# Attention of a two-layer encoder: a score tile's exponential issued as three instructions, one for each PSUM bank

## The chip, the cores and the metric

The kernel runs on one core of one Trainium2 chip. The metric is the device time of one execution in microseconds (us). Engines are named as the profile names them: PE is TensorE (PEld its weight loads), ACT is ScalarE, DVE is VectorE, POOL is GpSimd, SP is SyncE, which issues the DMAs.

## What is computed

The model takes 1024 tokens of width 1024, puts 16 meta tokens ahead of them, and runs two layers: a mixer of Fourier transform and attention with a squared-ReLU MLP, then an HGRN2 mixer with a second such MLP. The change touches the attention of the first layer alone. Cut to that, the reference is:

```python
N_Q_HEADS, N_KV_HEADS, HEAD_DIM = 6, 2, 128
q = apply_rope(rms_norm(q, q_gain), cos, sin)      # 1040 tokens, 6 heads
k = apply_rope(rms_norm(k, k_gain), cos, sin)      # 1040 tokens, 2 heads
s = jnp.einsum('bqhgd,bkhd->bhgqk', qb, k).astype(jnp.float32) * scale
p = jax.nn.softmax(s, axis=-1).astype(v.dtype)
o = jnp.einsum('bhgqk,bkhd->bqhgd', p, v)
```

Every query sees all 1040 keys. Everything is float32.

## The kernel before, in words

The sequence is padded to T = 1044 = 3 x 348 columns (CB = 348) and to nine token blocks of TT = 116. Matrix products are made of float32 values split into a high and a low part (fp32r), three passes each: high x high, high x low, low x high. The order of work is written out by hand for each engine, with semaphores between them; there is no scheduler.

**Tiles of the attention.** A tile g is one block of 116 queries of one head against all keys: 6 x 9 = 54 tiles. Its scores fill three PSUM banks (`ps[:, 0..2]`, 348 columns each, the last 4 of the last bank masked). Step s of block b works on tile g = 6b + s. Each engine has its own `attend(b, s)`: steps of block 0 are written out, blocks 1 to 8 are a loop, block 9 empties the pipeline. `begun` and `drained` leave out what does not exist yet or any more. In one step the engines issue, in this order:

- PE (line 1310): waits for the exponential of tile g - 1 (line 1318), then 9 score matmuls of tile g, three to a bank, a signal after each bank (`a_s`, lines 1319 to 1324). Then 9 matmuls of probabilities x values of older tiles into banks 6 and 7 (line 1336). Then, after the wait for the scaled probabilities of tile g - 1 (`a_p`, line 1342), 9 transposes of tile g - 1 into banks 3 to 5, three to a bank (line 1347); from the second tile on each bank first waits until the low part of tile g - 2 has been taken out of it (`a_pl`, line 1345).
- DVE (line 871): `low(0)`, the low part of bank 3 of tile g - 2 (line 876), which waits for ACT's `high(0)` of that bank (`a_ph`). Then the maximum of each score bank (line 885, waits `a_s`), two one-column instructions that make the exponent's bias (lines 887 and 890, signal `a_nb`), `low(1)` and `low(2)`, in steps 1 and 4 the low part of a new query group (line 869), and last the reciprocal of the tile's sum (line 897), which waits for the exponential (line 896).
- ACT (line 564): the exponential of tile g, one instruction over the three banks into `prob`, whose row sum goes to `amax[:, 5]` (lines 573 and 574, waits `a_nb`). It shows in the trace as an ACTIVATE and an ACTIVATION_READ_ACCUMULATOR; the signal `a_exp` is on the second. Then `high(0)` of tile g - 1 (line 579, waits `a_t`), the scaling of `prob` by the reciprocal (line 585, waits `a_rc`, signals `a_p`), `high(1)` and `high(2)`, and in some steps one more copy (line 591 in steps 2 and 5, line 562 in steps 0 and 3).

So `high(0)` stands behind the exponential on ACT, and the first maximum stands behind `low(0)` on DVE. POOL and SP do nothing in this stage: the weights of the next one are already there.

The few lines that matter most:

```python
A(prob[s % 2][0:TT, :].rearrange("p (a b) -> p a b", b=CB), ps[0:TT, 0:3, 0:CB], ACT.Exp, bias=amax[0:TT, 4:5],
  scale=scale_of(qsc, b, s), accum_out=amax[0:TT, 5:6]).then_inc(a_exp, 1)
```

`bias` and `scale` are both columns in SBUF, one value for each partition.

Of the kernel before, what the change touches and what calls it, by code (L numbers as in the profile page):

```python
# [17 lines left out]
F32 = mybir.dt.float32  # L18
F32R = mybir.dt.float32r
U8 = mybir.dt.uint8  # L20
ALU = mybir.AluOpType
ACT = mybir.ActivationFunctionType
AX = mybir.AxisListType

P = 128
# [5 lines left out]
CB = 348  # L31
T = 3 * CB
TT = T // 9
# [42 lines left out]
def encoder(nc, x, meta, mix_gain, ab_w_in, q_gain, k_gain, ab_w_out, c_w_in, lb_logits, o_gain,  # L76
# [3 lines left out]
    with ctx:  # L80
# [4 lines left out]
        def at(name, shape, dt, offset):  # L85
            return nc.alloc_sbuf_tensor_at(name, shape, dt, offset=base + offset, align_bytes=4)
# [14 lines left out]
        o_c = o_t + 4 * row  # L101
# [5 lines left out]
        stat = at("stat", [P, 2, 9], F32, o_c + 1484)  # L107
        qsc = at("qsc", [P, NQ, 9], F32, o_c + 1484 + 72)
        nqsc = at("nqsc", [P, NQ, 9], F32, o_c + 1484 + 72 + 216)
        amax = at("amax", [P, 8], F32, o_c + 1484 + 72 + 432)  # L110
        e_c = o_c + 1484 + 72 + 432 + 32


        xst = at("xst", [P, 9, 1024], F32, o_x)
# [17 lines left out]
        prob = (at("prob0", [P, T], F32, o_x + 9216 + 50176), at("prob1", [P, T], F32, o_t + 9216))  # L132
# [35 lines left out]
        ps = ctx.enter_context(nc.psum_tensor("ps", [P, 8, 512], F32))  # L168

        def sem(name):  # L170
            return ctx.enter_context(nc.semaphore(name))
# [62 lines left out]
        a_mn = sem("two_banks_bias_ready")  # L234
        a_nb = sem("exp_bias_ready")
        a_exp = sem("exp_done")
        a_rc = sem("sum_inverse_ready")
        a_p = sem("probs_ready")
        a_t = sem("probs_transposed")
# [89 lines left out]
        def group_col(b, kv):  # L329
            return b * CB + kv * (GRP * T)  # L330

        def scale_of(table, b, s):

            flat = table[0:TT, :, :].rearrange("p a b -> p (a b)")
            return flat[:, bass.ds(b * 3 + ((s // 3) * GRP * 9 + s % 3), 1)]

        def begun(b, s, lag):

            return not isinstance(b, int) or b * 6 + s >= lag

        def drained(b, s, lag):

            return isinstance(b, int) and b * 6 + s - lag >= 3 * NG

        def tile_cols(t, s):

            return t[0:TT, (s // 3) % 2, :, (s % 3) * TT:(s % 3 + 1) * TT]

        def turned(r):
            return ps[0:TT, 3 + r, 0:3 * TT].rearrange("p (a b) -> p a b", b=TT)  # L350
# [131 lines left out]
        def _(act):  # L482
            A = nc.scalar.activation
# [50 lines left out]
            for jj in range(8):  # L534
# [17 lines left out]
              bias=eps[0:TT, :], scale=1.0 / HD).then_inc(r_qr, 1)  # L552
# [7 lines left out]
            def q_high(b, gg):  # L560

                A(qh[:, gg, :], yf[:, bass.ds(group_col(b, gg), CB)], ACT.Copy).then_inc(a_qh, 1)

            def attend(b, s):

                g = b * 6 + s
                if not drained(b, s, 0):

                    act.wait_ge(a_nb, g + 1)
                    if begun(b, s, 2):  # L570

                        act.wait_ge(a_t, b * 18 + (3 * s - 3))
                    A(prob[s % 2][0:TT, :].rearrange("p (a b) -> p a b", b=CB), ps[0:TT, 0:3, 0:CB], ACT.Exp, bias=amax[0:TT, 4:5],  # L573
                      scale=scale_of(qsc, b, s), accum_out=amax[0:TT, 5:6]).then_inc(a_exp, 1)

                def high(r):
                    if begun(b, s, 1) and not drained(b, s, 1):
                        act.wait_ge(a_t, b * 18 + (3 * s - 2 + r))
                        A(tile_cols(pth, s - 1)[:, 3 * r:3 * r + 3, :], turned(r), ACT.Copy).then_inc(a_ph, 1)

                high(0)
                if not drained(b, s, 0):

                    act.wait_ge(a_rc, g + 1)
                    A(prob[s % 2][0:TT, :], prob[s % 2][0:TT, :], ACT.Copy, scale=amax[0:TT, 6:7]).then_inc(a_p, 1)
                high(1)
                high(2)
                if s in (2, 5) and begun(b, s, 8):

                    act.wait_ge(a_pv, b * 2 + (s // 3 - 1))  # L590
                    A(yf[:, bass.ds(group_col(b - 1, s // 3), CB)], ps[:, 6 + s // 3, 0:CB], ACT.Copy).then_inc(a_ev, 1)
                if s in (0, 3) and not drained(b, s, 0):

                    q_high(b + s // 3, 1 - s // 3)
# [3 lines left out]
            for s in range(6):  # L598
                attend(0, s)
            with act.Fori(1, 9) as b:  # L600
                for s in range(6):
                    attend(b, s)
# [128 lines left out]
        def _(dve):  # L731
            V = nc.vector
# [79 lines left out]
            for ft in range(2):  # L812
                dve.wait_ge(f_b, 2 * ft + 2)
                for hm in range(2):
                    c = ps[:, ((5, 6), (1, 2))[ft][hm], :]
                    s = bsin[:, ft, hm, :]
# [54 lines left out]
            def attend(b, s):  # L871
                def low(r):
                    if begun(b, s, 2) and not drained(b, s, 2):
                        hi, lo = tile_cols(pth, s - 2), tile_cols(ptl, s - 2)
                        dve.wait_ge(a_ph, b * 18 + (3 * s - 5 + r))
                        V.tensor_tensor(lo[:, 3 * r:3 * r + 3, :], turned(r), hi[:, 3 * r:3 * r + 3, :], ALU.subtract).then_inc(a_pl, 1)

                low(0)
                if not drained(b, s, 0):


                    col = [amax[0:TT, c:c + 1] for c in range(8)]
                    for c in range(3):
                        dve.wait_ge(a_s, b * 18 + (3 * s + c + 1))
                        V.tensor_reduce(col[c], ps[0:TT, c, 0:CB], AX.X, ALU.max).then_inc(a_mx, 1)
                    dve.wait_ge(a_mx, b * 18 + (3 * s + 2))
                    V.scalar_tensor_tensor(col[3], col[0], col[1], scale_of(nqsc, b, s), ALU.max, ALU.mult).then_inc(a_mn, 1)
                    dve.wait_ge(a_mx, b * 18 + (3 * s + 3))
                    dve.wait_ge(a_mn, b * 6 + (s + 1))
                    V.scalar_tensor_tensor(col[4], col[2], scale_of(nqsc, b, s), col[3], ALU.mult, ALU.min).then_inc(a_nb, 1)  # L890
                low(1)
                low(2)
                if s in (1, 4) and not drained(b, s, 0):
                    q_low(b + s // 4, 1 - s // 4)
                if not drained(b, s, 0):
                    dve.wait_ge(a_exp, b * 6 + (s + 1))
                    V.reciprocal(col[6], col[5]).then_inc(a_rc, 1)


# [265 lines left out]
        def _(pe):  # L1165
# [144 lines left out]
            def attend(b, s):  # L1310

                gg, i = s // 3, s % 3
                if not drained(b, s, 0):
                    if i == 0:
                        pe.wait_ge(a_ql, b * 2 + (gg + 1))
                    if begun(b, s, 1):

                        pe.wait_ge(a_exp, b * 6 + s)
                    for c in range(3):
                        n = CB if c < 2 else CB - (T - TOK)  # L1320
                        for q, k in ((qh, kh), (qh, kl), (ql, kh)):
                            ins = M(ps[0:TT, c, 0:n], q[:, gg, i * TT:(i + 1) * TT], k[:, gg, c * CB:c * CB + n],  # L1322
                                    start=(q is qh and k is kh), stop=(q is ql))
                        ins.then_inc(a_s, 1)

                p = (s - 2) % 3
                if begun(b, s, 5 + p) and not drained(b, s, 5 + p - 2):
                    jg, jb = ((s - 5 - p) // 3) % 2, (s - 5 - p) // 6
                    if p == 0:
                        pe.wait_ge(a_pl, b * 18 + 3 * (s - 2))  # L1330
                        if begun(b, s, 5 + 6):

                            pe.wait_ge(a_ev, (b + jb) * 2 + (jg - 1))
                    for c in range(3 * p, 3 * p + 3):
                        for v, w in ((vth, pth), (vth, ptl), (vtl, pth)):
                            ins = M(ps[:, 6 + jg, 0:CB], v[0:TT, jg * 9 + c, :], w[0:TT, jg, c, :], start=(c == 0 and v is vth and w is pth),
                                    stop=(c == 8 and v is vtl))
                    if p == 2:
                        ins.then_inc(a_pv, 1)
                if begun(b, s, 1) and not drained(b, s, 1):  # L1340

                    pe.wait_ge(a_p, b * 6 + s)
                    for r in range(3):
                        if begun(b, s, 2):
                            pe.wait_ge(a_pl, b * 18 + (3 * s - 5 + r))
                        for j in range(3 * r, 3 * r + 3):
                            ins = nc.tensor.transpose(ps[0:TT, 3 + r, (j % 3) * TT:(j % 3 + 1) * TT], prob[(s - 1) % 2][0:TT, j * TT:(j + 1) * TT], ident[0:TT, 0:TT])
                        ins.then_inc(a_t, 1)
# [289 lines left out]
```

## Time and profile before

| what | value |
|---|---|
| time, median of 3 runs | 3040.42 us (3037.49 to 3046.72) |
| the profiled execution: its time | 3046.08 us |
| its span in the profile | 3044.3 us |
| PE busy | 2865.9 us, 94% of the span |
| DVE busy | 1500.1 us, 49% |
| ACT busy | 690.5 us, 23% |
| POOL busy | 921.4 us, 30% |
| attention (first scores to last copy) | 240.5 to 476.3 us of the span |

The profile is one execution on the chip. Busy shares are averages over stages with different limits; the attention is 8% of the span. Starts are us from the span's start. An instruction's duration runs from its start to its end; the next one on the same engine can start before that end, so the distance between two starts is what an engine's queue really costs. Matmul ends are modelled.

### The profile page before, as it was taken

How to read it: one execution, taken by the hardware profiler on the slowest of the kernel's cores; microseconds unless marked ns; L12 is line 12 of the kernel's file. 1: busy time of each engine (PE TensorE's matmuls, PEld its weight loads, DVE VectorE, ACT ScalarE, POOL GpSimd, SP SyncE). 2: the span in 40 equal slices, each digit the busy share in tenths (PEclk: the TensorE clock that was granted, in tenths of full speed). 3: DMA queues.
4: the chain of work that ended last, by engine and by line, in shares of the span. 5: the costliest groups of instructions: out<-in, count | busy, mean ns of one | idle time of the engine just before them, and what ended most of it. 6: DMA issues, size and time to landing. Idle time of an engine off the chain costs nothing.

```text
span 3044.3 us, 40709 instructions
## 1 busy us (share of the span) xinstructions
PE 2865.9 (94%) x16501; PEld 2630.7 (86%) x16501; DVE 1500.1 (49%) x1832; ACT 690.5 (23%) x968; POOL 921.4 (30%) x396
## 2 busy tenths in 40 slices
PE   7998999999999999998999998998778999999998
PEld 6897999999999999998888888897766888888887
DVE  6377885431222222356867767768655322222224
ACT  3117883210000110121221221221223111000012
POOL 2230002343434434332222222222113444444442
PEclk9998999999999999999999999999888999999999
DMA  4010001111111111110000000000001111111111
GB/s 144 28 35 1 0 0 28 44 47 49 43 49 49 42 49 46 45 51 27 28 28 28 28 28 28 26 29 24 18 14 28 49 49 48 45 44 48 49 49 70
DMA packets 169438, 116.79 MB, mean 38 GB/s; under 512 B 3715, under 2 KB 163797, under 8 KB 169335
## 3 DMA queue, kind: packets, MB, share of 16 engines
q1 hardware_dynamic: 169190, 114.70, 12.5%
q8 instruction: 87, 1.43, 0.2%
q10 hardware_dynamic: 144, 0.53, 0.1%
q14 instruction: 17, 0.13, 0.0%
HBM read 111.03 MB, written 4.19 MB: 38 GB/s over the span
## 4 chain that ended last, share of the span: by engine, by line
PE 79%; DVE 12%; issue 5%; ACT 2%; DMA 0%; SPq 0%; DVEq 0%; ACTq 0%
PE ps L1196 67%; PE ps L1322 3%; PE ps L1461 3%; PE ps L1416 2%; DVE aa L1029 1%; DVE kk L1049 1%; PE ps L1484 1%; DVE h L922 1%; DVE kk L1048 1%; PE ps L1428 1%; ACT prob L573 1%; PE ps L1272 1%; DVE fd L1056 1%; DVE qq L1052 1%; DVE tmp L785 0%
## 5 line engine op out<-in xcount | busy, mean ns | idle before, releaser
L1196 PE MATMUL ps<-xh,wsp 128*128 128x348 f32 (+1 forms) x5056 | 1068.3, 340 | 18.2 <-DVE xl L771 12.2
L469 POOL TENSOR_TENSOR wsp<-raw,ones 128x1024 fp32r<-128x1024 f32 x196 | 387.5, 1977 | 2068.6 <-PE ps L1196 2049.2
L1196 PEld LDWEIGHTS ps<-xh,wsp 128*128 128x128 f32 x5056 | 860.9, 190 | 69.1 <-issue 18.6
L1196 PE MATMUL ps<-xl,wsp 128*128 128x348 f32 (+1 forms) x2528 | 593.6, 338 | 0.0
L1196 PE MATMUL ps<-ah,wsp 128*128 128x348 f32 (+1 forms) x2560 | 567.4, 350 | 0.0
L471 POOL TENSOR_TENSOR wsp<-raw,wsp 128x1024 fp32r<-128x1024 f32 x196 | 533.8, 2723 | 15.4
L1196 PEld LDWEIGHTS ps<-ah,wsp 128*128 128x128 f32 x2560 | 444.0, 188 | 44.7
L1196 PEld LDWEIGHTS ps<-xl,wsp 128*128 128x128 f32 x2528 | 441.4, 190 | 23.0
L1196 PE MATMUL ps<-al,wsp 128*128 128x348 f32 (+1 forms) x1280 | 323.1, 350 | 0.0
L618 ACT ACTIVATE tmp<-tmp 128x1044 f32<-128x1044 f32 (+1 forms) x64 | 68.5, 1071 | 1099.5 <-DVE tmp L939 559.0
L922 DVE TENSOR_TENSOR h<-h,ps 128x1024 f32<-128x1024 f32 x128 | 154.9, 1219 | 246.9 <-PE ps L1196 245.3
L1196 PEld LDWEIGHTS ps<-al,wsp 128*128 128x128 f32 x1280 | 225.7, 188 | 23.2
L923 DVE TENSOR_TENSOR h<-h,ps 128x1044 f32<-128x1044 f32 x72 | 89.3, 1240 | 256.5 <-PE ps L1196 256.5
L939 DVE SCALAR_TENSOR_TENSOR tmp<-ps,rms 128x1044 f32<-128x1044 f32 x32 | 39.9, 1246 | 278.2 <-PE ps L1196 275.4
L1461 PE MATMUL ps<-qq,kp 128*128 128x128 f32 (+1 forms) x960 | 136.8, 296 | 40.6 <-DVE qq L1052 26.1
L1461 PEld LDWEIGHTS ps<-qq,kp 128*128 128x128 f32 (+1 forms) x960 | 126.8, 201 | 52.8 <-issue 22.3
L937 DVE SCALAR_TENSOR_TENSOR tmp<-ps,rms 128x1024 f32<-128x1024 f32 x32 | 39.2, 1225 | 265.6 <-PE ps L1196 262.8
L679 ACT ACTIVATE kp<-kk 128x520 f32<-128x520 f32 (+1 forms) x112 | 66.5, 643 | 383.6 <-PE ps L1461 203.8
L943 DVE TENSOR_TENSOR al<-tmp,ah 128x1044 fp32r<-128x1044 f32 (+1 forms) x64 | 151.8, 2372 | 2.9 <-ACT ah L620 1.9
L1196 PE MATMUL ps<-oh,wsp 128*128 128x512 f32 x256 | 89.4, 452 | 39.6 <-DVE h L922 34.6
L1029 DVE COPY_PREDICATED aa<-msk,ps 128x512 f32<-128x512 uint8 x168 | 92.4, 589 | 53.6 <-PE ps L1461 52.6
L1196 PEld LDWEIGHTS ps<-oh,wsp 128*128 128x128 f32 x256 | 50.9, 212 | 62.0 <-DVE h L922 45.9
(181 smaller groups left out, 2986.4 us busy)
## 6 DMA issues: line engine op xcount, KB each, us to landing
raw<-in_w SPq DMA_DIRECT2D x128, 512.0 KB, 4.0
raw<-in_c_w_in SPq DMA_DIRECT2D x40, 512.0 KB, 3.7
raw<-in_ab_w_in SPq DMA_DIRECT2D x12, 512.0 KB, 3.8
xst<-in_x SPq DMA_DIRECT2D x8, 512.0 KB, 7.6
raw<-in_ab_w_out SPq DMA_DIRECT2D x8, 512.0 KB, 3.7
raw<-in_c_w_out SPq DMA_DIRECT2D x8, 512.0 KB, 3.2
out<-ost SPq DMA_DIRECT2D x16, 256.0 KB, 3.5
tabs<-in_dft_tok SPq DMA_DIRECT2D x2, 856.4 KB
```

The lines of the kernel that those rows point to most:

```text
L469: nc.gpsimd.tensor_tensor(wsp[:, slot, 0, :], raw[:, slot, :], one, ALU.mult).then_inc(w_high, 1)
L471: nc.gpsimd.tensor_tensor(wsp[:, slot, 1, :], raw[:, slot, :], wsp[:, slot, 0, :], ALU.subtract).then_inc(w_split, 1)
L618: A(tmp[:, j % 2, t0:t1], tmp[:, j % 2, t0:t1], ACT.Square).then_inc(l_s, 1)
L679: ins = A(dst, src, ACT.Copy)
L922: return V.tensor_tensor(real_pieces(h[:, k, :]), real_pieces(h[:, k, :]), real_outp(s), ALU.add).then_inc(z_free, 1)
L923: return V.tensor_tensor(pieces(h[:, k, :]), pieces(h[:, k, :]), outp(s), ALU.add).then_inc(z_free, 1)
L943: V.tensor_tensor(al[:, c0, j, t0:t1], tmp[:, j % 2, t0:t1], ah[:, c0, j, t0:t1], ALU.subtract).then_inc(l_l, 1)
L1029: V.copy_predicated(aa[0:rows, c0:c0 + n, 0:rows], mask, bank).then_inc(h_le, 1)
L1196: ins = M(ps[:, 3 * s + c, 0:n], w(a, k), b(k)[:, c0:c0 + n], start=(k == first and a == 0 and b is xa), stop=(k == last and a == 1))
L1322: ins = M(ps[0:TT, c, 0:n], q[:, gg, i * TT:(i + 1) * TT], k[:, gg, c * CB:c * CB + n], start=(q is qh and k is kh), stop=(q is ql))
L1416: ins = M(dst, left, right, start=(b == 0), stop=(b == len(parts) - 1))
L1461: ins = M(ps[0:n, 6 + (r0 + r) % 2, a * P:a * P + n], left, right, start=True, stop=True)
```

## The change

The one exponential of a tile becomes three, one for each bank of 348 columns, each with a sum of its own (columns 7 to 9 of `amax`, which grows from 8 to 10 columns). Each of them signals `a_exp`, so the semaphore counts 18 in a block, not 6. PE waits ahead of each bank of scores for the exponential of the same bank of the tile before. DVE waits for the third exponential, adds the three sums into column 5 with a new reduction, signals a new semaphore `a_sm`, waits for it, and then takes the reciprocal.

```diff
--- before.py
+++ after.py
@@ -107,8 +107,8 @@
         stat = at("stat", [P, 2, 9], F32, o_c + 1484)
         qsc = at("qsc", [P, NQ, 9], F32, o_c + 1484 + 72)
         nqsc = at("nqsc", [P, NQ, 9], F32, o_c + 1484 + 72 + 216)
-        amax = at("amax", [P, 8], F32, o_c + 1484 + 72 + 432)
-        e_c = o_c + 1484 + 72 + 432 + 32
+        amax = at("amax", [P, 10], F32, o_c + 1484 + 72 + 432)
+        e_c = o_c + 1484 + 72 + 432 + 40
 
 
         xst = at("xst", [P, 9, 1024], F32, o_x)
@@ -234,6 +234,7 @@
         a_mn = sem("two_banks_bias_ready")
         a_nb = sem("exp_bias_ready")
         a_exp = sem("exp_done")
+        a_sm = sem("sum_of_banks_ready")
         a_rc = sem("sum_inverse_ready")
         a_p = sem("probs_ready")
         a_t = sem("probs_transposed")
@@ -570,8 +571,9 @@
                     if begun(b, s, 2):
 
                         act.wait_ge(a_t, b * 18 + (3 * s - 3))
-                    A(prob[s % 2][0:TT, :].rearrange("p (a b) -> p a b", b=CB), ps[0:TT, 0:3, 0:CB], ACT.Exp, bias=amax[0:TT, 4:5],
-                      scale=scale_of(qsc, b, s), accum_out=amax[0:TT, 5:6]).then_inc(a_exp, 1)
+                    for c in range(3):
+                        A(prob[s % 2][0:TT, c * CB:(c + 1) * CB], ps[0:TT, c, 0:CB], ACT.Exp, bias=amax[0:TT, 4:5],
+                          scale=scale_of(qsc, b, s), accum_out=amax[0:TT, 7 + c:8 + c]).then_inc(a_exp, 1)
 
                 def high(r):
                     if begun(b, s, 1) and not drained(b, s, 1):
@@ -879,7 +881,7 @@
                 if not drained(b, s, 0):
 
 
-                    col = [amax[0:TT, c:c + 1] for c in range(8)]
+                    col = [amax[0:TT, c:c + 1] for c in range(7)]
                     for c in range(3):
                         dve.wait_ge(a_s, b * 18 + (3 * s + c + 1))
                         V.tensor_reduce(col[c], ps[0:TT, c, 0:CB], AX.X, ALU.max).then_inc(a_mx, 1)
@@ -893,7 +895,9 @@
                 if s in (1, 4) and not drained(b, s, 0):
                     q_low(b + s // 4, 1 - s // 4)
                 if not drained(b, s, 0):
-                    dve.wait_ge(a_exp, b * 6 + (s + 1))
+                    dve.wait_ge(a_exp, b * 18 + (3 * s + 3))
+                    V.tensor_reduce(col[5], amax[0:TT, 7:10], AX.X, ALU.add).then_inc(a_sm, 1)
+                    dve.wait_ge(a_sm, b * 6 + (s + 1))
                     V.reciprocal(col[6], col[5]).then_inc(a_rc, 1)
 
 
@@ -1313,10 +1317,10 @@
                 if not drained(b, s, 0):
                     if i == 0:
                         pe.wait_ge(a_ql, b * 2 + (gg + 1))
-                    if begun(b, s, 1):
-
-                        pe.wait_ge(a_exp, b * 6 + s)
                     for c in range(3):
+                        if begun(b, s, 1):
+
+                            pe.wait_ge(a_exp, b * 18 + (3 * s - 2 + c))
                         n = CB if c < 2 else CB - (T - TOK)
                         for q, k in ((qh, kh), (qh, kl), (ql, kh)):
                             ins = M(ps[0:TT, c, 0:n], q[:, gg, i * TT:(i + 1) * TT], k[:, gg, c * CB:c * CB + n],
```

## Rows read from the trace of the kernel before

**Rows 1.** Window from third to last exponential: PE, PEld, DVE, ACT, POOL busy; PEclk, DMA

```profile
254.36:465.45 211.09, 203.88 (x1355) 188.40 (x1356) 174.38 (x477) 185.96 (x338) 0.00 (x0) 1.00 0.00 0
```

**Rows 2.** Waits between 265 and 465 us: engine, line, releaser: us, times, longest

```profile
DVE amax L897 <- ACT prob L573: 23.7, 48, 0.7
ACT prob L573 <- DVE amax L890: 23.4, 48, 0.8
PEld ps L1322 <- ACT prob L573: 15.0, 48, 0.4
```

**Rows 3.** Timeline of ACT, one step: start, us, engine, line, operation

```profile
332.96 1.22 ACT L573 ACTIVATE prob<-ps,amax,qsc 116x1044 f32<-116x1044 f32 x1 [0.35 <-DVE amax L890]
334.08 0.19 ACT L573 ACTIVATION_READ_ACCUMULATOR prob<-ps,amax,qsc 116x1 f32 x1
334.17 0.45 ACT L579 ACTIVATE pth<-ps 116x348 fp32r<-116x348 f32 x1
334.51 1.17 ACT L585 ACTIVATE prob<-prob,amax 116x1044 f32<-116x1044 f32 x1
335.58 0.80 ACT L579 ACTIVATE pth<-ps 116x348 fp32r<-116x348 f32 x2
336.25 0.50 ACT L562 ACTIVATE qh<-y 128x348 fp32r x1
337.09 1.22 ACT L573 ACTIVATE prob<-ps,amax,qsc 116x1044 f32<-116x1044 f32 x1 [0.33 <-DVE amax L890]
```

**Rows 4.** Timeline of DVE, the same step

```profile
332.60 0.22 DVE L890 SCALAR_TENSOR_TENSOR amax<-amax,nqsc 116x1 f32<-116x1 f32 x1
332.74 0.94 DVE L876 TENSOR_TENSOR ptl<-ps,pth 116x348 fp32r<-116x348 f32 x2
334.30 0.16 DVE L897 RECIPROCAL amax<-amax 116x1 f32<-116x1 f32 x1 [0.62 <-ACT prob L573]
334.65 0.52 DVE L876 TENSOR_TENSOR ptl<-ps,pth 116x348 fp32r<-116x348 f32 x1 [0.19 <-ACT pth L579]
335.10 1.47 DVE L885 TENSOR_REDUCE amax<-ps 116x1 f32<-116x348 f32 x3
336.48 0.21 DVE L887 SCALAR_TENSOR_TENSOR amax<-amax,nqsc 116x1 f32<-116x1 f32 x1
336.73 0.22 DVE L890 SCALAR_TENSOR_TENSOR amax<-amax,nqsc 116x1 f32<-116x1 f32 x1
```

**Rows 5.** Timeline of PE, the same step

```profile
333.17 1.08 PE L1347 MATMUL ps<-ident,prob 116*116 116x116 f32 x9
334.32 0.42 PE L1322 MATMUL ps<-kh,qh 128*116 128x348 f32 x1
...
334.74 0.32 PE L1322 MATMUL ps<-kh,ql 128*116 128x348 f32 x1
...
335.69 0.32 PE L1322 MATMUL ps<-kh,ql 128*116 128x344 f32 x1
```

**Rows 6.** The chain that ended last, the start of the attention

```profile
244.50 1.32 ACT prob L573 x2
...
254.36 1.31 ACT prob L573 x2
...
259.83 0.36 ACT pth L579
260.21 0.52 DVE ptl L876
260.74 1.39 DVE amax L885 x3
```

**Rows 7.** Lines of ACT: instructions and durations in ns, min/median/max

```profile
L610 ACT ACTIVATE mh<-y x8: 1057/1058/1072, 476.3 to 483.1; 128x1044 fp32r<-128x1044 f32 x8
```

**Rows 8.** The same of line 562

```profile
L562 ACT ACTIVATE qh<-y x19: 473/503/505, 238.8 to 460.5; 128x348 fp32r x16, 128x348 fp32r<-128x348 f32 x3
```

**Rows 9.** Timeline of PE, transposes of the last tile

```profile
468.22 0.41 PE L1347 MATMUL ps<-ident,prob 116*116 116x116 f32 x2
```

## The prediction

> **What bounds the kernel now.** I asked first what a microsecond lost in this stage is worth. In the window from the third exponential to the last, POOL is idle, no DMA runs, and PE is busy 203.9 of 211.1 us at a granted clock of 1.00, the upper level of 2.4 GHz [rows 1]. Nothing from outside can be late here, the next stage's weights are there, and everything after it needs the attention: a step's gain or loss goes to the end undiminished. The window holds 51 distances between exponentials, 4.14 us each; in the step read below it is 337.09 - 332.96 = 4.13 us [rows 3].
>
> The list of waits gives the ring: DVE and PE wait for the exponential, the exponential waits for the bias [rows 2]. The timelines of the three engines place it. I count from the start E of an exponential (332.96).
>
> - ACT: E 0; sum read 1.12; high(0) 1.21, to 1.66; scaling 1.55; high(1) 2.62; a further copy 3.29 [rows 3].
> - DVE: reciprocal 1.34; low(0) 1.69, 0.03 after high(0) ends; first maximum 2.14; bias instructions 3.52 and 3.77; next exponential 4.13, 0.36 after the second [rows 3, 4].
> - PE: next scores at 1.36, 0.05 after the sum's read ends, and PE had been idle for 0.30, the average of the wait list (15.0/48) [rows 2, 3, 5].
>
> Two chains reach the first maximum together. By PE, bank 0 ends at 334.74 + 0.32 = 335.06. By ACT and DVE, exponential, high(0), low(0), and 0.44 later DVE is free: 335.09. The maximum starts at 335.10 [rows 4, 5]. After it PE is a little slower: its banks come 0.475 apart ((1.47 - 0.52)/2), while DVE left alone spaces maxima 0.435 ((1.39 - 0.52)/2), as in the chain at the stage's start, which indeed runs high, low, maximum [rows 4, 6]. So the PE chain bounds the step at 4.13, and **the ACT-DVE chain stands only 0.08 behind it, at 4.05**. The change frees the first and loads the second.
>
> **The change part by part.**
>
> *The wait of PE, bank by bank.* After the change bank 0 is released when the first sum is read, about E + 0.78. PE cannot use all of that: its transposes wait for low(1) and low(2), which end at 333.68, E + 0.72, and the last three follow; PE is free at 334.32 - 0.30, E + 1.06 [rows 4, 5]. The scores start 0.30 earlier. Bank 2 is released at about E + 2.02 and PE reaches it at 1.06 + 1.06 = 2.12: no wait. Gain on the PE chain 0.30 us, on the step at most the 0.08.
>
> *The exponential in three.* The elements are the same, two more instructions and two more sum reads come. An ACT instruction costs 0.84 ns for an element, from copies of 1044 and 348 columns: (1058 - 473)/696 [rows 7, 8]. From exponential to sum read are 1.12 us, less 1044 x 0.84 = 0.88: 0.24 fixed; from the read to the next start 0.09 [rows 3]. Two more: 2 x (0.24 + 0.09) = 0.67 us. All of it stands ahead of high(0), which starts at E + 1.88. Bounds of the fixed part: with the 503 ns of the loop's copies the slope is 0.80 and the fixed part 0.29, together 0.76; with the 450 ns of high(0), which reads PSUM as the exponential does, 0.87 and 0.21, together 0.60 [rows 3, 7, 8]. The low extreme is two high copies 0.35 apart, only 0.06 more than their elements [rows 3]: 0.30 together. I take 0.67, since the exponential has its own row. A gain is excluded: ACT only gets more to do.
>
> On this price the Trainium skill ("ScalarE: Activation LUTs", What ACT_TABLE_LOAD costs) says that an ACTIVATE with a bias column has about 280 ns beside its elements, one more such column adds 93, and neighbours overlap by 93. By that the fixed part is 0.28, the sum of the change +34 us and the time 3074; the page gives 1.24 us for our exponential and the row shows 1.22, so they agree. It is a rule against this change, and it also gives a reason for the 0.24.
>
> *The added reduction and its wait.* The third sum is ready at E + 1.97; the reduction starts at 2.00. A reduction of three elements is not in the trace: below it lies the reciprocal, 0.16, above it the one-column 0.21 of the bias and far above the 0.52 of a 348-column maximum [rows 4]. I take 0.17. The reciprocal then starts at 2.20, and low(0) can follow 0.14 later, as low(1) does after the bias: 2.34 [rows 4]. It would wait for high(0) until 1.88 + 0.45 + 0.03 = 2.36 anyway. Its cover is thus thin: with 0.21 it costs 0.02 a step, 1 us in all, with 0.52 it costs 0.34, 17 us.
>
> *What is queued behind.* On ACT the scaling moves from E + 1.55 to 2.41, high(1) to 3.48, high(2) to 3.82, the further copy to 4.16; ACT is free by about 4.55. PE's transposes need the scaled tile from E + 3.93 at the earliest and have it at 3.57. On DVE low(0) moves from 1.69 to 2.36, and the first maximum with it.
>
> *The new step.* 4.13 + 0.67 - 0.08 = 4.72 us: low(0) at 2.36, maxima from 2.80 spaced 0.435, bias, next exponential. It is the ACT-DVE chain, 4.05 + 0.67. ACT is free at 4.55, PE's own work is 4.13 - 0.30 = 3.83: neither bounds. 51 x 0.59 = **+30.0 us**.
>
> *Both ends.* From the first exponential to the third (9.86 us [rows 6]) there is no high or low yet, and the scores gain up to 0.6 in each of two distances; but the scaled tile, 0.86 later, holds the transposes ahead of the third scores. I take -0.4, between -1.2 and +0.5. At the end the last tile's transposes (468.22 [rows 9]) wait for its scaling, 0.86 later: +0.8. Sum: 30.0 - 0.4 + 0.8 = **+30.4 us**. The profiled execution took 3046.1 us, so its like would take 3076.5; the median shown is 5.7 below it, and against it I forecast 3040.4 + 30.4 = 3070.8.
>
> **The rivals.**
>
> *Serial sums.* An exponential that accumulates might not start until the sum before has been read: 0.19 after the read's start and not 0.09. No row shows two accumulating instructions in a row. Two gaps, +0.20 a step, +10: 3081.
>
> *Cheap pieces.* If the fixed part hides behind the piece before, as between two high copies, the pieces add 0.30: (0.30 - 0.08) x 51 = +11: 3051. Against it: the exponential's 0.24 is itself measured between starts.
>
> *PE sets the pace.* PE's row says that it waits 0.30 in each step for the exponential and for nothing else; freed, the step would be 3.83: -0.30 x 51 - 1 = -16, 3024. It decides where high(0) comes less than 0.08 later than now; and even with no delay at all the ACT-DVE chain stops the gain at 0.08 a step, -4. It would need my reading of rows 4, low(0) just ahead of the maximum, to be an accident of timing. Against it: the order on DVE is fixed in the code, and the chain at the start runs that way [rows 6].
>
> *The signals come together.* If the early exponentials' signals reached PE only with the third, the change would not do what it says. Scores at 2.02, banks again spaced by PE: 4.80 a step, +34, 3075. It lies within the main case's range.
>
> *The clock.* PE will idle 0.9 of 4.7 us, in one gap before its second group of transposes. If the clock fell to 1.2 GHz in this stage, the 3.83 would double: +3 us a step, at worst 150. Against it: the clock is 1.00 throughout the window, whose first steps have no value matmuls at all, 18 matmuls and not 27 [rows 1].
>
> **How the numbers follow.** The main case has 0.76 with the joined signals, its own range 3067 to 3076; serial sums 0.10; cheap pieces 0.07; PE's pace 0.03; the clock or something not seen, 0.04. The range takes in main case and serial sums with the spread of the runs (3037 to 3047) about them: 3059 to 3085. A measurement tells 0.3% from no change, 9 us. Slower 0.92 (main, serial, most of cheap pieces, clock), same 0.05, faster 0.03.
>
> **What the profile after would show.** Each exponential 0.64 us long, starts 0.63 apart; high(0) 1.88 after the first; the reduction about 0.17; low(0) at 2.36, directly ahead of the maxima, now 0.435 apart; exponentials of neighbouring tiles 4.72 apart. PE's wait ahead of the scores gone, and a new one of about 0.85 ahead of its transposes, for DVE's line 876. I am wrong if the first sum read comes before E + 0.45 or the next exponential starts over 0.15 after it, if low(0) waits for the reciprocal and not for high(0), or if the granted clock leaves 1.00.

## The result

| | before | changed |
|---|---|---|
| median, first comparison | 3041.93 us (3037.49 to 3046.72, 4 runs) | 3080.78 us (3077.23 to 3084.12, 4 runs) |
| ratio | | 1.0127, 95% interval 1.0111 to 1.0143 |
| median, second comparison | 3040.15 us (17 runs) | 3073.92 us (3069.01 to 3076.84, 4 runs) |
| ratio | | 1.0111, 95% interval 1.0090 to 1.0131 |
| span of the profiled execution | 3044.3 us | 3081.0 us |

The change makes the kernel slower, by 39 us in the first comparison and by 34 us in the second. The forecast was 3071, 30 us slower, with a range from 3059 to 3085.

One step of the changed kernel on ACT, from E = 338.25. It answers to [rows 3].

```profile
338.25 0.64 ACT L575 ACTIVATE prob<-ps,amax,qsc 116x348 f32<-116x348 f32 x1 [0.42 <-DVE amax L892]
338.79 0.19 ACT L575 ACTIVATION_READ_ACCUMULATOR prob<-ps,amax,qsc 116x1 f32 x1
338.88 0.63 ACT L575 ACTIVATE prob<-ps,amax,qsc 116x348 f32<-116x348 f32 x1
...
340.03 0.20 ACT L575 ACTIVATION_READ_ACCUMULATOR prob<-ps,amax,qsc 116x1 f32 x1
340.12 0.46 ACT L581 ACTIVATE pth<-ps 116x348 fp32r<-116x348 f32 x1
340.65 1.17 ACT L587 ACTIVATE prob<-prob,amax 116x1044 f32<-116x1044 f32 x1
...
342.93 0.64 ACT L575 ACTIVATE prob<-ps,amax,qsc 116x348 f32<-116x348 f32 x1
```

The pieces last 0.64 us and start 0.63 apart; the sum read comes 0.54 after each start and the next instruction 0.09 later. `high(0)` starts at E + 1.87, not at 1.21, and the next exponential at 4.68, not 4.13.

The same step on DVE [rows 4]:

```profile
340.26 0.16 DVE L899 TENSOR_REDUCE amax<-amax 116x1 f32<-116x3 f32 x1 [1.29 <-ACT prob L575]
340.45 0.16 DVE L901 RECIPROCAL amax<-amax 116x1 f32<-116x1 f32 x1
340.61 0.52 DVE L878 TENSOR_TENSOR ptl<-ps,pth 116x348 fp32r<-116x348 f32 x1
341.05 1.36 DVE L887 TENSOR_REDUCE amax<-ps 116x1 f32<-116x348 f32 x3
...
342.57 0.22 DVE L892 SCALAR_TENSOR_TENSOR amax<-amax,nqsc 116x1 f32<-116x1 f32 x1
```

Reduction at E + 2.01, reciprocal at 2.20, `low(0)` at 2.36 and the maxima directly behind it, 0.42 apart ((1.36 - 0.52)/2). DVE paces itself from `low(0)` on.

The timeline of PE in the same step [rows 5]:

```profile
338.60 0.94 PE L1351 MATMUL ps<-ident,prob 116*116 116x116 f32 x6 [0.53 <-DVE ptl L878]
339.31 0.39 PE L1326 MATMUL ps<-kh,qh 128*116 128x348 f32 x1
...
342.29 0.46 PE L1351 MATMUL ps<-ident,prob 116*116 116x116 f32 x3
343.28 0.94 PE L1351 MATMUL ps<-ident,prob 116*116 116x116 f32 x6 [0.53 <-DVE ptl L878]
```

And the list of waits of the changed kernel between 265 and 495 us, which answers to [rows 2]:

```profile
DVE amax L899 <- ACT prob L575: 55.7, 48, 1.4
PEld ps L1351 <- DVE ptl L878: 36.0, 47, 0.9
...
ACT prob L575 <- DVE amax L892: 11.3, 24, 1.0
DVE ptl L878 <- ACT pth L581: 2.5, 7, 0.4
```

The scores start at E + 1.06, as forecast, and hardly ever wait for an exponential any more (2.3 us in the whole stage, against 15.0). In their place PE waits 0.77 us a step (36.0/47) in the middle of its transposes, for the low parts of line 878. The wait has changed its name and more than doubled. Little of `high(0)` shows in the list, because DVE's reciprocal ends at 340.61 and `high(0)` at 340.58: DVE is held by the two together and is never seen idle for the second alone.

The granted clock did not stay at 1.00 from the third exponential to the last, as it had in the kernel before [rows 1]:

```profile
251.77:494.96 243.19, 213.51 (x1359) 188.08 (x1359) 177.12 (x528) 225.50 (x543) 0.00 (x0) 0.99 0.00 0
```

The lower level (1.2 GHz) falls into the first steps alone: 0.85 between 255 and 270 us, 1.00 from 270 us on.

Where the time is, by parts of the two profiles:

| part | before, us | changed, us | difference |
|---|---|---|---|
| first scores to first exponential | 4.0 | 4.0 | 0 |
| tiles 0 to 6 (six distances) | 26.4 | 28.8 | +2.4 |
| tiles 6 to 53: 40 steps within the loop | 4.13 each | 4.68 each | +22.2 |
| the 7 steps across the loop's end among them | 4.21 each | 5.13 each | +6.4 |
| last exponential to the copies of the next stage | 10.9 | 11.8 | +0.9 |
| **attention** | **235.8** | **267.7** | **+31.9** |
| MLP and the rest up to the second mixer | 858.5 | 858.3 | -0.2 |
| HGRN2 mixer | 935.6 | 942.0 | +6.4 |

31.9 us lie in the attention. Another 6.4 are the mixer's, which the change does not touch (see the second profile, below). What lies ahead of the attention, untouched too, was 1.5 us shorter (239.0 for 240.5), so the spans differ by 36.7.

### The profile page after: what moved, and what is told of

Its sections match the earlier page's. It is cut to its first block, busy times and chain, and to the rows that moved or that the text cites. A ratio compares the mean times of both kernels' runs of the same rounds, so it can differ in the third digit from the quotient of the medians.

```text
span 3081.0 us, 41043 instructions
## 1 busy us (share of the span) xinstructions
PE 2879.5 (93%) x16501; PEld 2630.0 (85%) x16501; DVE 1501.9 (49%) x1886; ACT 732.6 (24%) x1184; POOL 919.3 (30%) x396
## 4 chain that ended last, share of the span: by engine, by line
PE 79%; DVE 14%; issue 4%; ACT 2%; DMA 0%; SPq 0%; DVEq 0%; ACTq 0%
PE ps L1200 67%; PE ps L1465 3%; PE ps L1326 2%; DVE amax L887 2%; PE ps L1420 2%; PE ps L1351 1%; DVE aa L1033 1%; DVE kk L1053 1%; DVE h L926 1%; PE ps L1488 1%; DVE kk L1052 1%; DVE ptl L878 1%; ACT prob L575 1%; DVE qq L1056 1%; PE ps L1432 1%
## 5 line engine op out<-in xcount | busy, mean ns | idle before, releaser
L472 POOL TENSOR_TENSOR wsp<-raw,wsp 128x1024 fp32r<-128x1024 f32 x196 | 532.4, 2716 | 15.4
```

Of the source, the lines that this page charges most:

```text
L472: nc.gpsimd.tensor_tensor(wsp[:, slot, 1, :], raw[:, slot, :], wsp[:, slot, 0, :], ALU.subtract).then_inc(w_split, 1)
```

## The experiments

Starts are again counted from the first exponential of a step, E. "Attention" is the time from the first scores to the first copy of the next stage (line 610 in the kernel before), 235.8 us before and 267.7 after the change. Times are medians, set against the kernel before in the same comparison: 3040.78 us (23 runs) for the first four experiments, 3040.15 us (17 runs) for the others. The steps across the loop's end are those between two turns; the eight turns give seven of them.

### One wait of PE instead of three

```diff
+                    if begun(b, s, 1):
+                        pe.wait_ge(a_exp, b * 18 + 3 * s)
                     for c in range(3):
-                        if begun(b, s, 1):
-
-                            pe.wait_ge(a_exp, b * 18 + (3 * s - 2 + c))
```

> The changed kernel with one thing undone: PE waits once, for the third exponential of the tile before, as it did for the only one. Theory (the step is set by ACT and DVE: exponentials, high, low, maxima): the scores start at E + 2.03 (the third sum read ends at 1.98) instead of 1.05, the first maximum stays at 2.80, but the maxima then follow PE's banks, 0.475 apart and not 0.43: 4.78 us a step for 4.68, +0.10 in 43 steps, nothing in the 8 at the loop's end. About +4 us on the changed kernel: 3085. That is all that the waits by bank are worth. Rival (the waits by bank disturb PE and are part of the loss): faster than the changed kernel, 3075 or less. Rival (PE's earlier start is worth much and the loss would be far larger without it): +0.3 or more a step, 3095 or more.

Measured: 3082.2 us, +41.4 on the kernel before (1.0132, 1.0111 to 1.0152). By the times it can't be told from the changed kernel (3080.8 us); the rows tell them apart. Steps of 4.79, and 5.13 across the loop's end. The row of its first score matmul in PE's timeline, in the step with E = 338.61:

```profile
340.62 0.42 PE L1325 MATMUL ps<-kh,qh 128*116 128x348 f32 x1 [0.74 <-ACT prob L575]
```

And its maxima in DVE's timeline, in the same step:

```profile
341.39 1.47 DVE L887 TENSOR_REDUCE amax<-ps 116x1 f32<-116x348 f32 x3
```

The scores start 0.95 later than in the changed kernel, at 2.01, and the step pays 0.11 for it: the first maximum stands at 2.78 (2.80 in the changed kernel), and only the maxima's spacing goes from 0.42 to 0.48 ((1.47 - 0.52)/2). That is all that the finer waits are worth once the exponential is in pieces. The attention took 276.8 us, 9 more than in the changed kernel and not 4: five lie between tiles 0 and 6, where the granted clock was lower. The window of this kernel from its first exponential to its seventh (columns: stretch, its length, then busy us and instructions of PE, PEld, DVE, ACT and POOL, the granted clock as a share of 2.4 GHz, DMA):

```profile
236.70:270.84 34.14, 26.35 (x117) 23.16 (x118) 20.20 (x58) 24.86 (x60) 0.00 (x0) 0.64 0.00 0
```

The same window of the changed kernel:

```profile
243.00:271.82 28.82, 22.01 (x120) 18.75 (x120) 19.27 (x58) 24.86 (x60) 0.00 (x0) 0.88 0.00 0
```

0.64 against 0.88. PE idles for long in these steps in both kernels (7.8 and 6.8 us), which have few matmuls of probabilities and values or none. Whether the single wait or the spread between executions made the difference, one profile of this kernel can't tell.

### The added reduction alone

```diff
-                      scale=scale_of(qsc, b, s), accum_out=amax[0:TT, 5:6]).then_inc(a_exp, 1)
+                      scale=scale_of(qsc, b, s), accum_out=amax[0:TT, 7:8]).then_inc(a_exp, 1)
...
                     dve.wait_ge(a_exp, b * 6 + (s + 1))
+                    V.tensor_reduce(col[5], amax[0:TT, 7:10], AX.X, ALU.add).then_inc(a_sm, 1)
+                    dve.wait_ge(a_sm, b * 6 + (s + 1))
                     V.reciprocal(col[6], col[5]).then_inc(a_rc, 1)
```

The two columns beside the sum hold zeros.

> The kernel before with one exponential, and the added reduction over three columns (two of them zero) with its semaphore alone. Theory: the reciprocal starts at E + 1.53 instead of 1.34, low(0) could follow at 1.67 and waits for high(0) until 1.69 anyway: steps of 4.13 as before. At the loop's end DVE's branch stands between reciprocal and low(0) (0.41 to 0.55 us there): those 8 steps get 0.2 to 0.3 longer. Together +2 us: 3044. Rival (reduction and wait lie on the step's path): 0.2 in each of 53 steps, +10: 3052.

Measured: 3043.0 us, +2.2 (1.0011, 1.0001 to 1.0020); attention 238.1 us, +2.3. Steps of 4.125 as before, 4.46 across the loop's end instead of 4.21. These seven account for 1.7 us; most of the rest lies in the first distance of all, 5.35 for 4.50 us. The timeline of DVE in an ordinary step (E = 322.54):

```profile
323.87 0.16 DVE L899 TENSOR_REDUCE amax<-amax 116x1 f32<-116x3 f32 x1 [0.63 <-ACT prob L574]
324.06 0.16 DVE L901 RECIPROCAL amax<-amax 116x1 f32<-116x1 f32 x1
324.22 0.52 DVE L878 TENSOR_TENSOR ptl<-ps,pth 116x348 fp32r<-116x348 f32 x1
```

And in one across the loop's end (E = 334.93):

```profile
336.44 0.16 DVE L901 RECIPROCAL amax<-amax 116x1 f32<-116x1 f32 x1
336.96 0.52 DVE L878 TENSOR_TENSOR ptl<-ps,pth 116x348 fp32r<-116x348 f32 x1 [0.35 <-ACT pth L580]
```

In the ordinary step `low(0)` starts 0.16 after the reciprocal, at E + 1.68, as before. Across the loop's end 0.52 lie between the two: DVE's branch stands there (its row is shown under "Why the prediction was right"). So the reduction costs nothing in the ordinary steps of the kernel before, where PE sets the pace; it costs 0.25 at each of the seven loop ends.

### A spare copy ahead of `high(0)`, or ahead of `high(2)`

```diff
                 def high(r):
                     if begun(b, s, 1) and not drained(b, s, 1):
                         act.wait_ge(a_t, b * 18 + (3 * s - 2 + r))
+                        if r == 0:
+                            if begun(b, s, 2):
+                                act.wait_ge(a_dm, b * 6 + (s - 1))
+                            A(rot[0:TT, 0:CB].rearrange("p (a b) -> p a b", b=TT), turned(r), ACT.Copy).then_inc(a_dm, 1)
                         A(tile_cols(pth, s - 1)[:, 3 * r:3 * r + 3, :], turned(r), ACT.Copy).then_inc(a_ph, 1)
```

The second kernel has `r == 2` in the added line. `a_dm` is a new semaphore; ACT waits for its last count ahead of the next stage.

> The kernel before, with one spare ACT copy of 348 columns in each step, just ahead of high(0), into memory that nobody reads. It costs ACT 0.34 us. Theory: high(0), low(0) and the first maximum come 0.34 later; that chain stood 0.08 behind PE's, so the step becomes 4.39: +0.26 in 43 steps, +0.18 in the 8 at the loop's end, which have a bubble to cover: +12.6 us, 3054.5. Rival (what counts is ACT's load, wherever it stands): the same as the spare copy behind, whatever that is. Rival (PE's wait for the exponential sets the step, the high and low parts do not): no change, 3042.

Measured: 3059.3 us, +18.5 (1.0061, 1.0045 to 1.0078); steps of 4.37, attention 249.1 us, +13.3. The attention agrees with the theory's +12.6, but the times lie above it: +12.6 is 1 us below their interval's lower end, +13.7. The profiled execution is the fastest of the five. ACT's timeline in the step with E = 332.04, the spare copy and `high(0)`:

```profile
333.26 0.45 ACT L583 ACTIVATE rot<-ps 116x348 f32<-116x348 f32 x1
333.60 0.46 ACT L584 ACTIVATE pth<-ps 116x348 fp32r<-116x348 f32 x1
```

DVE's timeline, `low(0)` and the maxima:

```profile
334.10 0.52 DVE L882 TENSOR_TENSOR ptl<-ps,pth 116x348 fp32r<-116x348 f32 x1 [0.54 <-ACT pth L584]
334.53 1.36 DVE L891 TENSOR_REDUCE amax<-ps 116x1 f32<-116x348 f32 x3
```

`low(0)` has gone from 1.69 to 2.06, and the maxima follow it without a gap, 0.42 apart.

> The kernel before, with the same spare ACT copy just ahead of high(2). Theory: high(2) ends at E + 3.76, low(2) needs it at 4.34; ACT is free at about 4.0 and the next exponential is due at 4.13: no change, 3042 (3040 to 3044). Rival (ACT's load counts): +0.34 in each step, up to +17, 3059, or the same as the copy ahead.

Measured: 3042.4 us, +1.6 (1.0002, 0.9989 to 1.0014); steps of 4.12, attention 236.4 us. ACT at the end of the step with E = 327.44:

```profile
330.39 0.46 ACT L583 ACTIVATE rot<-ps 116x348 f32<-116x348 f32 x1
330.73 0.47 ACT L584 ACTIVATE pth<-ps 116x348 fp32r<-116x348 f32 x1
...
331.56 1.22 ACT L574 ACTIVATE prob<-ps,amax,qsc 116x1044 f32<-116x1044 f32 x1
```

The same instruction with the same 0.34 us of ACT time costs 13 us in one place and nothing that shows in the other. This is the experiment that decides between the theory and ACT's load: what counts in this kernel is what stands between the exponential and `high(0)`.

### Two pieces instead of three

```diff
-                    for c in range(3):
-                        A(prob[s % 2][0:TT, c * CB:(c + 1) * CB], ps[0:TT, c, 0:CB], ACT.Exp, bias=amax[0:TT, 4:5],
-                          scale=scale_of(qsc, b, s), accum_out=amax[0:TT, 7 + c:8 + c]).then_inc(a_exp, 1)
+                    for i, (c0, c1) in enumerate(((0, 2), (2, 3))):
+                        A(prob[s % 2][0:TT, c0 * CB:c1 * CB].rearrange("p (a b) -> p a b", b=CB), ps[0:TT, c0:c1, 0:CB], ACT.Exp, bias=amax[0:TT, 4:5],
+                          scale=scale_of(qsc, b, s), accum_out=amax[0:TT, 7 + i:8 + i]).then_inc(a_exp, 1)
```

PE waits ahead of banks 0 and 2, and the reduction adds two sums.

> The exponential in two instructions, banks 0 and 1 together and bank 2 alone, with a wait of PE ahead of bank 0 and of bank 2, and the added reduction over two sums; everything else as in the changed kernel. Theory (fixed part and sum read of each further piece delay high(0)): one further piece, 0.33 us; high(0) at E + 1.55, low(0) at 2.03, step 4.05 + 0.33 = 4.38 (0.25 more than before in 43 steps) and about 4.75 at the loop's end (0.5 more in 8, for DVE's branch and the reduction): +15 us, 3056. Rival (the loss comes from splitting as such, whatever the number): near the changed kernel, 3080.

Measured: 3059.1 us, +18.9 (1.0060, 1.0044 to 1.0076); steps of 4.35, 4.80 across the loop's end, attention 252.6 us, +16.7. ACT in the step with E = 328.72:

```profile
328.72 0.93 ACT L575 ACTIVATE prob<-ps,amax,qsc 116x696 f32<-116x696 f32 x1 [0.42 <-DVE amax L892]
...
330.26 0.45 ACT L581 ACTIVATE pth<-ps 116x348 fp32r<-116x348 f32 x1
...
333.07 0.93 ACT L575 ACTIVATE prob<-ps,amax,qsc 116x696 f32<-116x696 f32 x1
```

`high(0)` at 1.54, 0.33 later than with one piece; with three it was 0.66 later. The price goes by the piece.

### The same two pieces in another order

```diff
+                for i, (c0, c1) in enumerate(((0, 2), (2, 3))):
+                    if not drained(b, s, 0):
+                        A(prob[s % 2][0:TT, c0 * CB:c1 * CB].rearrange("p (a b) -> p a b", b=CB), ps[0:TT, c0:c1, 0:CB], ACT.Exp, bias=amax[0:TT, 4:5],
+                          scale=scale_of(qsc, b, s), accum_out=amax[0:TT, 7 + i:8 + i]).then_inc(a_exp, 1)
+                    if i == 0:
+                        high(0)
+                high(1)
+                high(2)
                 if not drained(b, s, 0):
                     act.wait_ge(a_rc, g + 1)
                     A(prob[s % 2][0:TT, :], prob[s % 2][0:TT, :], ACT.Copy, scale=amax[0:TT, 6:7]).then_inc(a_p, 1)
-                high(1)
-                high(2)
...
                     for c in range(3):
+                        if c == 1:
+                            inverse()
                         dve.wait_ge(a_s, b * 18 + (3 * s + c + 1))
```

`inverse()` is the reduction and the reciprocal of tile g - 1, taken from the end of DVE's step.

> The two pieces again, reordered: on ACT high(0) between the two exponentials, high(1) and high(2) ahead of the scaling; on DVE reduction and reciprocal of the last tile between the first and the second maximum of the next one. The same instructions, no more and no fewer. Theory: low(0) at E + 1.40 is off the path; PE is free at 1.06 and its first bank ends at 1.80; reduction and reciprocal push the later maxima back by 0.3, so the next exponential is due at about 4.10, and ACT, with the further copy in two of three steps, is free at 4.15. Steps of about 4.13, no loss at the loop's end: 3042 (3037 to 3047), 14 us under the same pieces in the old order. Rival (three engines' work has grown, so the order hardly matters): within 4 us of the two pieces in the old order.

Measured: 3045.6 us, +5.4 on the kernel before, not told apart from it (1.0007, 0.9994 to 1.0019), and 13.5 under the same pieces in the old order. Steps of 4.00 to 4.12, 4.38 across the loop's end; attention 233.6 us, 2.2 less than before. ACT's timeline in the step with E = 323.74:

```profile
323.74 0.93 ACT L582 ACTIVATE prob<-ps,amax,qsc 116x696 f32<-116x696 f32 x1 [0.20 <-DVE amax L906]
...
324.67 0.45 ACT L578 ACTIVATE pth<-ps 116x348 fp32r<-116x348 f32 x1
325.01 0.65 ACT L582 ACTIVATE prob<-ps,amax,qsc 116x348 f32<-116x348 f32 x1
...
327.82 0.92 ACT L582 ACTIVATE prob<-ps,amax,qsc 116x696 f32<-116x696 f32 x1
```

DVE's timeline in the same step, `low(0)`, the first maximum and the reciprocal:

```profile
325.15 0.52 DVE L880 TENSOR_TENSOR ptl<-ps,pth 116x348 fp32r<-116x348 f32 x1 [0.69 <-ACT pth L578]
325.59 0.52 DVE L901 TENSOR_REDUCE amax<-ps 116x1 f32<-116x348 f32 x1
...
326.21 0.16 DVE L889 RECIPROCAL amax<-amax 116x1 f32<-116x1 f32 x1
```

The last score matmul of the first bank, in PE's timeline:

```profile
325.23 0.32 PE L1334 MATMUL ps<-kh,ql 128*116 128x348 f32 x1
```

`high(0)` has come forward from 1.21 to 0.93, `low(0)` from 1.69 to 1.41 and the first maximum from 2.14 to 1.85. That maximum still stands directly behind `low(0)`, and PE's first bank is ready 0.04 before it (325.55): the two chains arrive together again, so `low(0)` is not off the path as the theory has it. ACT goes from one instruction to the next without a pause in this step, and between 265 and 455 us it waits for DVE's bias only 16 times, 3.4 us in all. This is the fastest attention of the study, by the profile, but the whole kernel's time shows no gain. The profiled execution, 3036.0 us, lies 9.6 us below the median of the eleven.

### The three pieces in that order

The same edit on the changed kernel, with `high(0)` after the first of three pieces.

> The changed kernel's three exponentials, reordered in the same way: high(0) after the first piece, high(1) and high(2) ahead of the scaling, reduction and reciprocal between the first and the second maximum of the next tile. Theory: the place of high(0) makes the loss, not the 0.67 us of ACT time; ACT then becomes the bound: 1.87 for the three pieces, 1.03 for the high copies, 1.07 for the scaling, 0.37 for the further copy in two of three steps: 4.34 in those, about 4.15 in the others, 4.28 on average: +0.14 in 51 steps, 3049 (3044 to 3056), some 30 us under the changed kernel. Rival (the ACT time itself is the loss): near 3080.

Measured: 3055.5 us, +15.4 (1.0049, 1.0031 to 1.0068); steps of 4.22 to 4.37, 4.38 across the loop's end; attention 244.0 us, +8.2 on the kernel before and 23 under the changed kernel's second profile. By the times it is 18 under the changed kernel, where some 30 were expected. The step with E = 328.51 on ACT:

```profile
328.51 0.64 ACT L582 ACTIVATE prob<-ps,amax,qsc 116x348 f32<-116x348 f32 x1
...
332.54 0.48 ACT L595 ACTIVATE y<-ps 128x348 f32 x1
332.88 0.67 ACT L582 ACTIVATE prob<-ps,amax,qsc 116x348 f32<-116x348 f32 x1
```

ACT is busy from end to end: 332.88 - 328.51 = 4.37. The steps are near the theory's (4.34 with a further copy, 4.15 without), and its +7 us is near the attention's +8. The whole time is higher than that, by an amount that the profiled execution (span 3048.3, only 4 above the profile before) does not show; why the timed runs lie higher stays open.

### The changed kernel once more

> The changed kernel unaltered, for a second profile and times on the same chip as the three others. In the first profile the attention was 32 us longer and the stage of the HGRN2 mixer 6 us longer, with 7 us more at TensorE's lower clock in it. Theory: attention again 32 us longer (steps of 4.68 and about 5.1 at the loop's end), the mixer's stage anywhere between 932 and 942 us, as in the profiles of kernels that differ from the one before by a copy. Rival (the change lengthens the later stage too): the mixer's stage again at 940 us or more.

Measured: 3073.9 us, +33.8. Steps of 4.68, 5.12 across the loop's end, attention 266.8 us, +31.0. The mixer's stage in the profiles of the kernel before, the changed kernel and this one (windows, columns as above). Before:

```profile
1334.80:2270.40 935.60, 835.55 (x5257) 776.85 (x5256) 639.53 (x834) 217.39 (x321) 221.98 (x90) 0.95 0.09 26
```

The changed kernel, first profile:

```profile
1365.00:2307.00 942.00, 839.38 (x5257) 778.53 (x5256) 640.28 (x833) 217.33 (x321) 220.36 (x90) 0.95 0.09 25
```

The changed kernel, second profile:

```profile
1358.80:2294.60 935.80, 836.18 (x5257) 776.79 (x5255) 637.32 (x833) 217.31 (x320) 221.34 (x90) 0.96 0.09 26
```

935.6, 942.0 and 935.8 us: the second profile of the changed kernel has none of the first one's 6 us. In the other seven kernels the stage took 931.8 to 940.7 us, in no order that follows the attention. It is a spread between executions; an effect of the change on it is not seen. The mixer's is not the only one: the stretch ahead of the attention, the same in all ten but for one small memset in the second experiment, took 233.2 to 240.5 us (239.0 and 233.8 in the two profiles of the changed kernel). That leaves 31 to 32 us for the change itself: within the interval of the second comparison (27 to 40 us), and 2 us below the lower end of the first (34 to 43 us). In the profiled execution of the first the mixer's 6.4 us came on top; the other timed runs have no profile.

## Why the prediction was right

- **The two chains.** The reading that the ACT-DVE chain stood 0.08 behind PE's is borne out: a delay of 0.34 ahead of `high(0)` cost 0.25 a step (4.37 for 4.125), the same 0.34 behind cost nothing.
- **The exponential in three.** The forecast fixed part of 0.24 and 0.09 for the read give starts 0.63 apart and `high(0)` at 1.88; the rows show 0.63 and 1.87. The Trainium skill ("ScalarE: Activation LUTs", What ACT_TABLE_LOAD costs) gives 0.28 for the fixed part, 0.04 above the row, and says nothing of the sum's read. The rival of serial sums is out: the next accumulating instruction starts 0.09 after the read's start, while that read still runs.
- **The reduction.** Forecast 0.17, measured 0.16, and free in the ordinary step of the kernel before, as its own experiment shows. `low(0)` stands at 2.36, as forecast. In the changed kernel it is a tie: DVE goes on to `low(0)` 0.16 after the reciprocal starts, which is when `high(0)` lets it go as well. The prediction would be wrong "if low(0) waits for the reciprocal and not for high(0)"; the rows can't tell the two apart, and by this reading a longer reduction would have cost time.
- **The step.** Forecast 4.72, measured 4.68. The difference is the spacing of the maxima and what follows them: from the first maximum to the next exponential 1.88 us, forecast 1.92. Over the 40 ordinary steps between tiles 6 and 53 that is 1.4 us less than forecast (22.2 for 23.6).
- **PE.** Scores at 1.06 and one gap before the second group of transposes, both as forecast. The rival that PE sets the pace is out, and so is that of signals which come together: even with a single late wait the step is only 0.11 longer.
- **The step that was missing** is the loop. The sum used 51 equal distances. Across the loop's end DVE's branch puts 0.52 us between reciprocal and `low(0)`; before, the wait for `high(0)` hid nearly all of it, 0.41 against the 0.35 of an ordinary step [rows 4]. The changed kernel moves the reciprocal by 0.86 and `high(0)` by 0.66, and the branch comes out: 5.13 us for 4.68. DVE's timeline at that place, in the kernel before:

```profile
292.91 0.16 DVE L897 RECIPROCAL amax<-amax 116x1 f32<-116x1 f32 x1 [0.63 <-ACT prob L573]
293.32 0.52 DVE L876 TENSOR_TENSOR ptl<-ps,pth 116x348 fp32r<-116x348 f32 x1 [0.24 <-ACT pth L579]
```

And in the changed kernel:

```profile
354.50 0.16 DVE L901 RECIPROCAL amax<-amax 116x1 f32<-116x1 f32 x1
355.02 0.52 DVE L878 TENSOR_TENSOR ptl<-ps,pth 116x348 fp32r<-116x348 f32 x1 [0.35 <-ACT pth L581]
```

Between the two starts 0.41 before and 0.52 after. `low(0)` is at E + 2.72 there (E = 352.30), 0.36 later than in an ordinary step. The other 0.08 of the 5.13 is not new: from the second bias instruction to the next exponential ACT needs 0.44 across the loop's end and 0.36 within it, which is why the kernel before has 4.21 there for 4.13. The branch itself, in the list of the loop's own instructions in the changed kernel (durations in ns, then first and last start):

```profile
L909 DVEq COMPARE_BRANCH  x8: 50/56/67, 297.5 to 497.2; - x8
```

The first of the eight, at 297.5, stands between a reciprocal at 297.40 and a `low(0)` at 297.94. The prediction priced the reduction's cover as thin, 0.02 a step, and did not ask what else used the same cover; the reduction alone already lets 0.25 of the branch out (4.46 for 4.21). What the steps across the loop's end lose beyond the ordinary ones is (0.92 - 0.55) x 7 = 2.6 us of the 31.9, and 2.3 us beyond the forecast's 0.59 a step. A loop with fewer turns was not tried.
- **The ends.** Forecast -0.4 and +0.8. At the start the first two distances shrank by 1.1 us (8.8 for 9.9) and the next four grew by 3.5, where 4 x 0.59 = 2.4 was forecast: +2.4 for the six against a forecast of +2.0. In the second profile the same parts gave -0.4 and +2.5. At the end +0.9.
- **The clock.** The prediction called itself wrong if the granted clock left 1.00, and it did, to 0.99. The four distances in which it fell are the 5.35, 4.65, 5.24 and 4.81 us behind the third exponential; in the second profile they were 5.00, 4.64, 4.65 and 4.81. So at most some 1.3 us of the 31.9 belong to it, an estimate from 5.35 and 5.24 against 4.65. The rival's collapse of the clock through the whole stage did not come.
- **The sum.** Forecast +30.4, in the attention +31.9 and +31.0. That it is so close is in part luck: the ordinary steps' 1.4 us too much and the 2.3 us of the loop that were missing nearly cancel. The times gave +39 and +34. The 7 and 3 above the attention's are within what the mixer's stage and the stretch ahead of the attention vary by from one profile to the next; where they lie in the timed runs is open.

The chance of 0.10 for serial sums, at 3081, would have been right on the first median for a wrong reason. Only the rows of the step tell the two apart.

## What to carry to other kernels

Where PE waits for the end of a long instruction, ask before cutting it up what else stands behind it on its own engine, and how far behind the second chain is: here 0.08 us of slack was all that there was to gain, and each further ACTIVATE with two column operands and a sum cost 0.33 us ahead of the instruction that fed that chain. If it has to be cut, put the urgent successor between the pieces and take as few pieces as will do. A step of an unrolled loop body and a step across the loop's end are different steps; cover that is measured in the first is not there in the second.

## What was not expected of the hardware

- A further exponential of 348 columns costs 0.33 us of ACT time beside its elements, also when it follows its like: the fixed part does not hide behind the piece before (0.63 between starts with 0.29 us of elements, three pieces or two).
- From the start of the instruction ahead of DVE's branch to the start of the one behind it are 0.41 to 0.54 us, of which the branch's own row has 0.06. Why it was 0.41 in one kernel and 0.52 in others is open.
- The mixer's stage, untouched by any of these kernels, took between 931.8 and 942.0 us in ten profiles; two profiles of one and the same kernel gave 942.0 and 935.8, the first at a granted clock of 0.95 and the second at 0.96. The stretch ahead of the attention took 239.0 us in the first, at 0.93, and 233.8 in the second, at 0.96.
